# State-space loop of a two-block transformer kernel: the four rotated products of a step move from POOL to DVE

## The reference

```
u = h @ w_in
bu_re, bu_im = u_c x bb_re, u_c x bb_im          # per group: 16 inputs -> 64 states
state(t) = lam * state(t-1) + bu(t)              # complex, per state, 256 tokens
y = Re(state) x c_re - Im(state) x c_im          # per group: 64 states -> 16 outputs
g = gelu(y + d * u);  g = g * sigmoid(g @ w_glu);  out = g @ w_out
```

## Time and profile before

| | |
|---|---|
| median of three runs | 2221.24 us (2218.53 to 2223.39) |
| the profiled execution, its own time | 2220.33 us |
| its span in the trace | 2218.5 us |
| the loop, first DVE instruction to the end of the last POOL product | 1220.15 to 1363.93 us |
| DVE in 1219 to 1371 us | busy 136.98 of 152.00 us |
| POOL in 1219 to 1371 us | busy 93.38 of 152.00 us |
| granted TensorE clock in 1219 to 1371 us | 0.81 |

### The profile page before, as it was taken

One profiled execution on the slowest core, in us unless ns is written; L12 is line 12 of the kernel. 1 busy time (PEld: TensorE's weight loads), 2 busy tenths in 40 slices (PEclk: granted clock), 3 DMA queues, 4 the chain that ended last, 5 costly groups with the idle time before them and its releaser, 6 DMA issues.

```text
span 2218.5 us, 24261 instructions
## 1 busy us (share of the span) xinstructions
PE 1838.9 (83%) x9254; PEld 1361.6 (61%) x9254; DVE 1440.6 (65%) x2651; ACT 558.3 (25%) x740; POOL 418.7 (19%) x342
## 2 busy tenths in 40 slices
PE   3698867777788778879998667999999989559999
PEld 2576553333333333349997556599989978436998
DVE  7884449888888888658764995255555554624554
ACT  1123010100000001024433100244444433124442
POOL 0020024444454444500000664000000000000000
PEclk9899988999998999999999788999999999769999
DMA  8471358999999999944553221444534544204553
GB/s 362 150 291 57 133 206 357 422 421 421 422 421 421 418 421 420 414 194 162 189 189 123 72 73 57 152 160 181 198 143 174 195 161 152 76 0 144 197 178 125
DMA packets 63852, 502.09 MB, mean 226 GB/s; under 512 B 7201, under 2 KB 7457, under 8 KB 11297
## 3 DMA queue, kind: packets, MB, share of 16 engines
q0 software_dynamic: 37008, 268.98, 29.3%
q1 hardware_dynamic: 25776, 229.40, 28.6%
q10 hardware_dynamic: 992, 2.74, 0.3%
HBM read 500.04 MB, written 1.05 MB: 226 GB/s over the span
## 4 chain that ended last, share of the span: by engine, by line
PE 56%; DVE 22%; DMA 15%; issue 3%; ACT 3%; POOL 1%; ACTq 0%; DVEq 0%; SPq 0%
PE PB L760 22%; DMA arena<-in_uv,eidx 12%; PE PB L771 10%; PE PB L744 6%; PE PB L544 4%; PE PB L876 3%; DVE arena L1318 2%; DMA ring<-in_uv,eidx 2%; DVE arena L1035 2%; DVE arena L1487 2%; PE PB L482 1%; PE PB L594 1%; PE PB L496 1%; PE PB L702 1%; PE PB L728 1%
## 5 line engine op out<-in xcount | busy, mean ns | idle before, releaser
L744 PE MATMUL PB<-arena 128*128 128x512 f32 x604 | 306.4, 665 | 119.0 <-DVE arena L1326 119.0
L760 PE MATMUL PB<-h_lo,gu_hi 128*128 128x256 f32 x1344 | 382.2, 284 | 0.0
L760 PE MATMUL PB<-h_hi,gu_hi 128*128 128x256 f32 x1344 | 375.1, 279 | 4.8 <-DVE gu_lo L1347 4.8
L760 PE MATMUL PB<-h_hi,gu_lo 128*128 128x256 f32 x1344 | 375.6, 279 | 0.0
L1888 POOL DMA_INDIRECT arena<-in_uv,eidx x193 | 228.0, 1181 | 434.7 <-PE PB L744 222.5
L744 PEld LDWEIGHTS PB<-arena 128*128 128x128 f32 x604 | 124.9, 212 | 300.5 <-DVE arena L1326 151.8
L1318 DVE CUSTOM_DVE_ANT_0 arena<-arena,XN 128x1024 f32<-128x1024 f32 x193 | 230.6, 1221 | 77.2 <-DMA arena<-in_uv,eidx 77.2
L760 PEld LDWEIGHTS PB<-h_hi,gu_hi 128*128 128x128 f32 x1344 | 252.6, 188 | 8.8 <-DVE gu_lo L1347 5.7
L760 PEld LDWEIGHTS PB<-h_lo,gu_hi 128*128 128x128 f32 x1344 | 252.6, 188 | 3.1
L760 PEld LDWEIGHTS PB<-h_hi,gu_lo 128*128 128x128 f32 x1344 | 252.4, 188 | 0.0
L1347 DVE TENSOR_TENSOR gu_lo<-ring,gu_hi 128x2048 fp32r<-128x2048 f32 x85 | 194.9, 2293 | 74.8 <-ACT gu_hi L1751 74.1
(11 more groups left out here) (339 smaller groups left out, 2977.0 us busy)
## 6 DMA issues: line engine op xcount, KB each, us to landing
ring<-in_ffn SPq DMA_DIRECT2D x88, 1536.0 KB, 6.5
arena<-in_ada SPq DMA_DIRECT2D x23, 768.0 KB, 7.4
ring<-in_qkv SPq DMA_DIRECT2D x12, 1024.0 KB, 4.8
ring<-in_zg SPq DMA_DIRECT2D x8, 1024.0 KB, 9.8
ring<-in_s5b SPq DMA_DIRECT2D x8, 1024.0 KB, 4.9
ring<-in_ada SPq DMA_DIRECT2D x4, 1536.0 KB, 13.8
ring<-in_up SPq DMA_DIRECT2D x4, 1024.0 KB, 5.2
ring<-in_wo SPq DMA_DIRECT2D x4, 1024.0 KB, 5.1
```

Source lines behind the costliest of these rows:

```text
L744: mm = pe.matmul(PB[2 + 2 * t + h][:, :], lhsT=diag(n), rhs=uv[n % UVB][:, 1, h * 512:(h + 1) * 512], start=False, stop=False, skip_group_ ...
L760: mm = pe.matmul(PB[j % 2][:, b * T:(b + 1) * T], lhsT=w[:, j % 2, o:o + P], rhs=h[:, k, :], start=(k == 0 and m == 0), stop=(k == DC - 1 ...
```

## The change

The four rotated products of a step are formed by DVE, behind the scans of the same step. POOL's loop is dropped. DVE waits for `y_full` ahead of the products, as POOL did, and tells `o_ready` with the fourth. Its wait for `o_ready` ahead of the scans goes, since DVE itself has read the set of `w` by then. PE's and ACT's lists are as they were. POOL's remaining work after the loop (a mask for the second layer) waits for a later semaphore, as before.

```diff
@@ DVE, in the loop over i
                 if i >= 2:
-                    dve.wait_ge(o_ready, i - 1)
                     dve.wait_ge(last_kept, min(2 * (i - 1), 16))
...
                         if b == 1 and j == 3:
                             tell(ins, w_ready)
+                if i >= 2:
+                    dve.wait_ge(y_full, i - 1)
+                wr, wi = (s5w[:, W_AT[i % 2] + b, :, :] for b in range(2))
+                o = [s5w[:, 4 + 4 * (i % 2) + k, :, :] for k in range(4)]
+                v.tensor_tensor(o[0], wr, ec, ALU.mult)
+                v.tensor_tensor(o[1], wi, es, ALU.mult)
+                v.tensor_tensor(o[2], wr, es, ALU.mult)
+                tell(v.tensor_tensor(o[3], wi, ec, ALU.mult), o_ready)
@@ POOL
-            for i in range(16):
-                q = i % 8
-                ec, es = Ec[:, 4 * q:4 * q + 4, :], Es[:, 4 * q:4 * q + 4, :]
-                if i == 0:
-                    pool.wait_ge(tab_ready, 2)
-                pool.wait_ge(w_ready, i + 1)
-                if i >= 2:
-                    pool.wait_ge(y_full, i - 1)
-                wr, wi = (s5w[:, W_AT[i % 2] + b, :, :] for b in range(2))
-                o = [s5w[:, 4 + 4 * (i % 2) + k, :, :] for k in range(4)]
-                g.tensor_tensor(o[0], wr, ec, ALU.mult)
-                g.tensor_tensor(o[1], wi, es, ALU.mult)
-                g.tensor_tensor(o[2], wr, es, ALU.mult)
-                tell(g.tensor_tensor(o[3], wi, ec, ALU.mult), o_ready)
```

## The result

The changed kernel takes 2228.72 us (median of 17 runs, 2225.95 to 2233.31), the kernel before 2221.45 us (median of 17, 2218.53 to 2227.4). The ratio is 1.0033 with a 95% interval of 1.0025 to 1.0042. In microseconds that is +7.3, with an interval of about +5.5 to +9.3. The forecast was +5.5 us, 2226.7, in a range of 2222.5 to 2231.0, slower with 0.72.

A forecast was written before the change was run, and what follows sets the result against it. DVE was taken to set the loop's pace, partly held out by POOL. Added products of 40.3 us, less 29.75 of stalls and 5.07 of POOL's products at the end, gave +5.5 us, 2226.7 us, range 2222.5 to 2231.0.

The forecast's parts named there:

- DVE paces the loop: In the loop, DVE waits once, 9.4 us ahead of step 0, and sets the pace; PE and ACT follow.
- Stalls returned: In steps 1 to 15, DVE gets back the time POOL's products held it out, 29.75 us.
- Tail: Behind the last scans, POOL's products of the last step, 5.07 us, go from the exposed path.
- Added block: Four products a step on DVE, all on the path: 2.52 us a step, 40.3 us in all.
- Waits at zero: In the loop, DVE's new wait for `y_full` and the `last_kept` wait cost nothing.
- The clock term: Last `s5_out`, behind the loop: left at 4.06 us, with -1.6 and +0.4 us kept for the range.
- Products at full length: Rival: DVE's new products don't overlap, 4.3 us more, +9.8 us, 2231.0 us; chance 0.04.
- products at the scans' pace: Rival: DVE's new products run at 0.33 us each, -12 us, 2209 us; chance of faster 0.03.
- stalls that aren't POOL's: Rival: DVE's stalls in the loop aren't given back by the change, +35 us, 2256 us; chance 0.02.
- Within the measurement: Rival: total within about 0.2% (4.4 us), as with a fast last `s5_out`, +3.9 us, 2225.1; chance 0.25.
- a full exchange: Rival: in the loop, time given back equals work moved, only 2.5 us of tail saved, 2218.7 us; chance 0.02.

The follow-up runs named there:

- e1: Kernel before, with POOL forming only the first two of its four products from step 2 on; 2196.75 us, ratio 0.9888 to the kernel before.
- e2: Kernel before, with the four products of step 15 alone formed by DVE; 2219.73 us, ratio 0.999 to the kernel before.
- e3: Changed kernel, with DVE forming the four products of every step twice; 2269.56 us, ratio 1.0213 to the kernel before.
- e10: Kernel before, with POOL's third and fourth product replaced by four copies of 512 elements; 2208.98 us, one run.
- e8: Kernel before, with DVE forming one product of a step and POOL the other three behind it; 2219.12 us, ratio 0.9985.
- e7: Changed kernel, with further matmuls on PE ahead of the last two `s5_out`; 2228.82 us, ratio 1.0029 to the kernel before.
- e5: Kernel before, with two products on DVE and two on POOL, POOL starting as soon as the scans are done; 2226.87 us, ratio 1.0019.
- e4: Kernel before, with two products on DVE, then two on POOL beside DVE's next products with a PSUM source; 2211.99 us, ratio 0.9952.
- e6: As e4, with all four products of step 15 on DVE; 2210.51 us, ratio 0.9951 to the kernel before.

## Why the prediction was right

**Step by step.** That DVE paces the loop held: the changed kernel's DVE waits for PE only ahead of step 0, 9.36 us as before. *Stalls returned* (29.75 us): confirmed by e1, and by the scans of 2.63 us in step 1 of the changed kernel. *Tail* (5.07 us of POOL's products gone, 2.5 of DVE's in their place): confirmed by e2 and by the chain. *Added block* (40.3 us): 2.53 us in the changed kernel and 40.49 us in e3. *Waits at zero*: none appeared. The sum of these terms, +5.5, measured +5.78 in the profiled executions; steps of 9.04 us in place of 9.03 and the like, times 16, make up the difference.

**Two readings to correct.** The 1.22 and 1.23 us for POOL's products alone are steps of the chain, from one start to the next; POOL's timeline gives them 1.26 us, and that is what 1.77 and 1.70 compare with. And POOL need not read two operands to keep DVE out: in e10 one is enough. Neither enters the sum.

**The clock term.** I left the last `s5_out` at 4.06 us although I expected PE to idle longer ahead of it, with +0.4 kept as a bound. PE idled 4.76 us ahead of it in place of 2.83, and it measured 4.50, the bound. With it the loop costs +6.23 us.

**The total.** The medians say +7.3, and the loop's +6.23 lies in their interval (+5.5 to +9.3). I can't place the remaining 1.1 us. The code ahead of the loop is the same in all kernels here, yet the loop began between 1219.00 and 1226.61 us in their profiles. In the changed kernel's profile it began 1.66 us later than in the one before, and the first dot product of the expert layer (L1318) had already begun at 335.4 in place of 333.5. Scatter of that size is enough for 1.1 us. In the eight other kernels with several runs, e1 to e8, the change in the median and the change in the profiled loop also differ, by -1.5 to +2.6 us. But the kernels with all products on DVE (changed, e3, e7) all lie on the same side, at +1.1, +0.8 and +2.6. It wasn't tested whether a part of it belongs to the change.

**The rivals.** Products at full length, products at the scans' pace, and stalls that aren't POOL's have fallen (e3, e3, e1). "Within the measurement" needed a fast last `s5_out`; e7 shows that this would have given +4.2 us in the loop, which is 0.2%. But the median of e7 is at 1.0029 [1.0018, 1.0039] with that fast group, so the clock of this one group would not by itself have brought the total to "within the measurement". The second way of that rival, a full exchange, has fallen: the stalls given back are 2.0 us a step and the block costs 2.53. The remark of the Trainium skill, "Perfetto Trace Analysis", section "Optimizing Scalar/DVE Operations", that offloading between the two engines might not help, fits e5, which is slower than the kernel before (1.0019), and not e4, which is 0.5% faster with the same shares of the work.

## What to carry to other kernels

An engine's long instruction in a timeline, next to a short one of the same form in another step, can be a stall in disguise; here taking away POOL's two products (e1) showed that it was. Price what an offload costs the engine that is helped from the step that runs without the helper, and compare that with the work it takes over. Here the exchange was 2.0 us of stall and 5.07 us once for 2.5 us of work a step, and moving everything back lost by little. The gain lay in neither extreme but in e4: as much of POOL's reading work as fits beside DVE instructions with a source in PSUM, started there by a semaphore. Where a kernel has such instructions, that is the place to try.

## What the runs showed of the hardware that was not expected

- A DVE instruction that is held out is longer by somewhat less than POOL's whole product: 1.07 us for DVE's difference L1469, where a POOL product lasts 1.26 us alone (step 15). POOL's products are longer too, 1.70 to 1.78 us in the kernel before. These lengths fit two engines that take turns, one instruction each, though no row shows the hand-over itself. A POOL copy with one source does the same (1.13 and 0.96 us in place of 0.62), a memset beside the same DVE instructions does not (0.95 us throughout).
- `s5_out` took 2.43 to 2.46 us at a granted clock of 1.00 and up to 4.50 at 0.50, and neither the idle time just ahead of it nor the group before decides by itself. In e6 3.67 us of idling was followed by 2.43 us, and 1.70 us by 4.46. In e2 0.45 us was followed by 2.46, right behind a group of 4.50 us; in e6 the slow last group also followed a slow one (4.47). What decides stays open.
